# Score and probability-value matmuls issued as runs, and the next group's attention laid over eight gate tiles instead of six

## What is computed

```python
xn = rms_norm(x, lp['norm_mix'])
proj = xn @ lp['w_in']                       # q | k | v | pool_in | two gates of 1024
q, k = per-head rms_norm of q, k
a = swa_prompt(q, k, v, lp['sinks'])         # 64-query chunks see their own and the 2 chunks before
pl = pool_mixer(p_ext, pos, lp['w_pool'], lp['pool_scale'])
ya = a @ lp['w_br_attn']
yb = pl @ lp['w_br_pool']
g = jax.nn.sigmoid(gates + lp['gate_bias'])
mix = (g[:, :, 0] * ya + g[:, :, 1] * yb) @ lp['w_out']
x = x + mix
x = x + conv_ffn(rms_norm(x, lp['norm_ffn']), ...)   # up 1024->5632, conv of 3, gelu * value, down
```

## Time and profile before

| | |
|---|---|
| median of 3 runs | 3370.05 us (3366.35 to 4027.73) |
| the profiled execution | 3370.61 us |
| its span, core 6 (the slowest) | 3369.1 us |
| spans of all cores | 3351.0 to 3369.1 us |
| busy shares on core 6 | PE 97%, DVE 63%, ACT 47%, POOL 30% |

### The profile page before, as it was taken

One profiled execution on the slowest core, in us unless ns is written; L12 is line 12 of the kernel. 1 busy time (PEld: TensorE's weight loads), 2 busy tenths in 40 slices (PEclk: granted clock), 3 DMA queues, 4 the chain that ended last, 5 costly groups with the idle time before them and its releaser, 6 DMA issues.

```text
span 3369.1 us, 53769 instructions; the slowest of 8 cores (3351.0 to 3369.1 us)
## 1 busy us (share of the span) xinstructions
PE 3284.3 (97%) x17681; PEld 1605.2 (48%) x17835; DVE 2138.3 (63%) x3379; ACT 1570.1 (47%) x2557; POOL 1010.9 (30%) x1151
## 2 busy tenths in 40 slices
PE   6899999999999999999998999999999999999999
PEld 3544444444444444444444444444445555555554
DVE  4655555647766866677656555556477666776665
ACT  3444444435444654446535444444265444564444
POOL 3232323114322433234333222221143332333312
PEclk8999999999999999999998999999999999999999
DMA  9556555346422333223562222222451222112211
GB/s 192 93 113 117 115 119 113 80 155 203 115 84 67 86 90 102 83 67 73 166 188 32 77 76 76 76 76 78 154 183 57 68 68 68 34 35 68 68 45 45
DMA packets 147474, 320.45 MB, mean 95 GB/s; under 512 B 26336, under 2 KB 85376, under 8 KB 140480
## 3 DMA queue, kind: packets, MB, share of 16 engines
q1 hardware_dynamic: 134128, 214.59, 20.6%
q0 software_dynamic: 6592, 56.79, 10.9%
q10 hardware_dynamic: 6480, 45.62, 3.9%
HBM read 304.18 MB, written 115.41 MB: 125 GB/s over the span
## 4 chain that ended last, share of the span: by engine, by line
PE 90%; DMA 3%; DVE 2%; issue 2%; ACT 1%; SPq 1%; POOL 0%; DVEq 0%; ACTq 0%; POOLq 0%
PE psb L626 89%; DMA xsl<-xT 2%; SPq L642 1%; DVE xn L635 1%; DMA sph<-sph 0%; PE psb L1127 0%; ACT psb L629 0%; DVE ug L635 0%; DMA xsl<-x 0%; ACT srt L629 0%; DVE PT L632 0%; DMA xsl<-xm 0%; ACT ug L629 0%; ACT L629 0%; DVE xsl L635 0%
## 5 line engine op out<-in xcount | busy, mean ns | idle before, releaser
L626 PE MATMUL psb<-xn,w_up 128*128 128x482 bf16 (+3 forms) x6336 | 1259.2, 362 | 0.0
L626 PEld LDWEIGHTS psb<-xn,w_up 128*128 128x128 bf16 x6336 | 619.9, 98 | 636.0
L632 POOL TENSOR_TENSOR actT<-ug,uv 128x480 bf16<-128x480 f32 (+3 forms) x360 | 425.1, 1181 | 1098.5 <-ACT ug L629 939.0
L635 DVE SCALAR_TENSOR_TENSOR ug<-psb,pv,ug 128x480 f32<-128x480 f32 (+3 forms) x792 | 557.4, 704 | 128.1 <-ACT ug L629 42.2
L626 PE MATMUL psb<-actT,w_dn 128*128 128x480 bf16 (+3 forms) x3168 | 631.3, 361 | 0.0
L635 DVE SCALAR_TENSOR_TENSOR uv<-psb,pv,uv 128x480 f32<-128x480 f32 (+3 forms) x792 | 557.0, 703 | 64.2 <-ACT uv L629 11.8
L629 ACT ACTIVATE ug<-psb,pv 128x480 f32<-128x480 f32 (+3 forms) x396 | 291.8, 737 | 535.0 <-PE psb L626 523.6
L626 PE MATMUL psb<-xn,w_eg 128*128 128x512 bf16 x1969 | 476.5, 382 | 8.1 <-issue 3.0
L626 PEld LDWEIGHTS psb<-actT,w_dn 128*128 128x128 bf16 x3168 | 310.0, 98 | 315.5
L629 ACT ACTIVATE uv<-psb,pv 128x480 f32<-128x480 f32 (+3 forms) x396 | 292.7, 739 | 199.1 <-PE psb L626 198.8
L632 POOL TENSOR_TENSOR sqx<-sqx,sqx 128x512 f32<-128x512 f32 (+5 forms) x238 | 287.7, 1209 | 204.3 <-ACT sqx L629 195.9
(11 more groups left out here) (166 smaller groups left out, 2537.9 us busy)
## 6 DMA issues: line engine op xcount, KB each, us to landing
wb<-wun POOLq DMA_DIRECT2D x42, 1024.0 KB, 9.8
xsl<-x SPq DMA_DIRECT2D x68, 512.0 KB, 6.2
xm<-xsl SPq DMA_DIRECT2D x64, 512.0 KB, 5.4
xsl<-xT SPq DMA_DIRECT2D x60, 512.0 KB, 6.9
w_up<-wb ACTq DMA_DIRECT2D x22, 1024.0 KB, 5.3
xsl<-xm SPq DMA_DIRECT2D x28, 482.0 KB, 6.8
xsl<-xm SPq DMA_DIRECT2D x28, 480.0 KB, 5.0
x<-xsl SPq DMA_DIRECT2D x28, 480.0 KB, 3.2
```

Of the source, the lines that this page charges most:

```text
L626: S.op("pe", lambda e: e.matmul(out=out, lhsT=lhsT, rhs=rhs, start=start, stop=stop), reads=reads, writes=writes)
L632: S.op(eng, lambda e: e.tensor_tensor(out=out, in0=a, in1=b, op=op), reads=reads, writes=writes)
L635: S.op("dve", lambda e: e.scalar_tensor_tensor(out=out, in0=a, scalar=s, in1=b, op0=op0, op1=op1), reads=reads, writes=writes)
```

## The change

Four things. (1) `mm_run` makes one operation of the list out of several matmuls: they are issued one behind the other, with the waits ahead of the first and the signal on the last. The two matmuls of an `att_S` pair (g = 0 and 1) become one run, and the 16 of `att_PV` another. (2) The planner gives such a run its own cost (`span`): 4n/2.4 + 10, which is 223 ns for n = 128, and 580 ns for the sixteen. (3) The planner knows two modes of PE: it adds 100 ns (`SWITCH`) when it goes from a half-row run to another kind of matmul or back, and while PE is in the half-row mode it takes a half-row run that is ready ahead of all others, wherever that stands in the list. (4) In the loop over groups `att_spread` takes the place of `att_steps`: `att_S` of tile i stands behind gate tile 2i, `att_PV` of tile i behind gate tile 2i+1, and `att_T` of tile i behind gate tile 2i+2, ahead of `att_S` of tile i+1. The last `att_T` falls behind gate tile 7: it stands after the `root` and `scales` of the norm of group i+2 and ahead of `stage_F`. The attention in `stage_B` at the start of each layer keeps `att_steps`, with its matmuls in runs.

```diff
+SWITCH, RUN_PV = 100, 580.0
...
+    if op.span is not None:
+        return op.span
...
-            pick = min((x for x in pend[e] if x[0] <= t), key=lambda x: x[1])
+            half = e == "pe" and halves
+            pick = min((x for x in pend[e] if x[0] <= t), key=lambda x: (half and not x[2].half, x[1]))
...
+            if e == "pe" and op.half != halves:
+                t += SWITCH
+                halves = op.half
...
+        def mm_run(mms, reads, writes, span, half=False):
+
+            def run(e):
+                for (out, lhsT, rhs, start, stop) in mms:
+                    ins = e.matmul(out=out, lhsT=lhsT, rhs=rhs, start=start, stop=stop)
+                return ins
+            o = S.op("pe", run, reads=reads, writes=writes)
+            o.span, o.half = span, half
...
-                for g in range(2):
-                    mm(psb[0:nk, b + g, 0:4 * n].rearrange("p (h q) -> p h q", h=4), kx[g * 64:(g + 1) * 64, 0:nk],
-                       G.q[0][g * 64:(g + 1) * 64, 0:4, col - G.qo:col - G.qo + n], True, True, [kr] + G.q[1], pr(b + g))
+                mms = [(psb[0:nk, b + g, 0:4 * n].rearrange("p (h q) -> p h q", h=4), kx[g * 64:(g + 1) * 64, 0:nk],
+                        G.q[0][g * 64:(g + 1) * 64, 0:4, col - G.qo:col - G.qo + n], True, True) for g in range(2)]
+                mm_run(mms, [kr] + G.q[1], pr(b, b + 1), 4 * n / 2.4 + 10, True)
...
+            mms = []
             for g in range(2):
                 for h in range(4):
...
-                    mm(o, PT[pi][:, 0, hc:hc + n], vp[:, g, 0:65], True, False, [f"PT{pi}_0", vpr], pr(b + g))
-                    mm(o, PT[pi][0:nkc, 1, hc:hc + n], vc[0:nkc, g, 0:65], False, True, [f"PT{pi}_1", vcr], pr(b + g))
+                    mms.append((o, PT[pi][:, 0, hc:hc + n], vp[:, g, 0:65], True, False))
+                    mms.append((o, PT[pi][0:nkc, 1, hc:hc + n], vc[0:nkc, g, 0:65], False, True))
+            mm_run(mms, [f"PT{pi}_0", f"PT{pi}_1", vpr, vcr], pr(b, b + 1), RUN_PV)
...
+        def att_spread(l, G):
+
+            A = G.att
+            steps = [[] for _ in range(2 * len(A) + 1)]
+            for i, a in enumerate(A):
+                steps[2 * i].append(lambda x=a: att_S(l, G, x))
+                steps[2 * i + 1].append(lambda x=a: att_PV(l, G, x))
+                steps[2 * i + 2].insert(0, lambda x=a: att_T(l, G, x))
+            return steps
...
-                steps = att_steps(l, nxt) if nxt is not None and not (l == 0 and i == 0) else []
+                steps = att_spread(l, nxt) if nxt is not None and not (l == 0 and i == 0) else []
...
                 if job is not None:
                     job.root()
                     job.scales()
+                for st in steps[KT:]:
+                    for s in st:
+                        s()
                 for g in Gs:
                     stage_F(l, g)
```

More of the change, by code:

```diff
@@ L33 @@
                  "waits", "signal", "sig", "K", "epoch", "gidx", "chain", "alias",
-                 "preds", "after", "succ", "left", "cost", "table", "size", "shared", "start", "end")
+                 "preds", "after", "succ", "left", "cost", "table", "size", "shared", "start", "end", "span", "half")
 class _Probe:
@@ L150, in op @@
         o.chain = None
+        o.span = None
+        o.half = False
         self.ops.append(o)
@@ L226, in arrange @@
         pend = {e: [] for e in self.ENGS}
-        table, busy = None, {}
+        table, busy, halves = None, {}, False
         lock = {"dve": 0.0, "pool": 0.0}
```

## The result

The changed kernel takes 0.9887 of the time before, with a 95% interval of 0.9858 to 0.9915: 3332 us where 3370 stood, 38 us less. Two of its four runs were slow, with one die at a lower clock, and are left out; the other two took 3328.98 and 3332.22 us. The forecast was 3336, 1.0% less; it is 1.1%. The profiled execution has spans of 3318.7 to 3327.4 us over the cores, where 3351.0 to 3369.1 stood.

The account below looks back on a forecast made before the run. The prediction took PE's issue to bound the gate stage of 14 mixer groups. From 3370.6 us it took 31.9 for whole runs of four and 2.5 for the layer starts, giving 3336 us, with a range of 3322 to 3356.

Parts of the forecast that it names:

- What bounds the kernel: Gate stage of 14 mixer groups: only PE counts, busy 82.99 of 83.00 us; whatever shortens its issue is saved whole.
- The prices: Score matmuls on PE: a run of one or two costs 0.42 us, of three or four 0.64, switches included.
- The second pair and its weights: Fours in the score runs: by the skill, second pairs would wait for weight loads, 5 us off the saving; trace decides.
- Why the scores were parted: Attention tiles 2 and 3: banks come free one by one, late in the planner's reckoning, so gate matmuls go between.
- Fours everywhere: The 14 groups: four runs of four each, 35.8 us where 67.7 stands, 31.9 us saved.
- The starts: Starts of the layers: layer 0 pairs save 2.5 us, layer 1's saving falls into waits; up to 5 us either way.
- Pairs without fours: Rival, score runs: each attention tile keeps two runs of one pair, saving 20.7 us, total 3347; chance 0.12.
- Evictions: Rival, gate stage: ACT and DVE run late after the scores, half the gain lost, 16 us, total 3352; chance 0.08.
- The last transpose: Rival, fourth tile's att_T: PE waits up to 6.4 us in each of 14 groups, total 3426; chance 0.04.

Follow-up runs that it names:

- one more switch: Kernel with each tile's four score matmuls in one run, plus a full-row matmul of 32 columns between its two pairs: 0.9924, 3337.2 us.
- a parted tile: Changed kernel with a full-row matmul of 32 columns between the two halves of each score pair, spread kept: 1.0008.
- fours forced on six steps: Changed kernel with each tile's four score matmuls in one run and att_steps instead of att_spread in the gate stage: 0.9916, 3348.7 us.
- The run of four: Changed kernel with both score pairs of each attention tile in one mm_run that waits for all four banks, spread kept: 0.9886, 3323.9 us.
- the first four experiments: Runs with six steps 0.9929; spread without runs 0.9896; kernel before without table load for exponentials 0.9986; changed kernel without planner's modes 0.9887.
- the next four: Four scores in one run 0.9886; that with a small matmul between pairs 0.9924; changed kernel with halves parted 1.0008, with sixteen single operations 0.9901.

## Why the prediction was right

**What bounds the kernel.** Right. PE was and is busy for all of a later group, and what its issue lost the time lost: of the 38 us of the ratio 35 lie in the 14 groups, and 30 of these are the count of runs.

**The prices.** Right, and shown by the kernels that changed little but the count: 0.42 and 0.64 us for a run gave 23.5 where 24 came (runs without spread), 15.5 where 13.3 came (one more switch, partly by luck), 1.31 where 1.30 came (a parted tile). The cleanest check is a later group of layer 0, where PE has no gaps. Against the changed kernel's 79.7 us the prices give 2.5 us more for the kernel before, 0.6 for the runs without the spread, 0.9 for one more switch and 2.7 for the parted halves; measured are 2.5, 0.6, 0.9 and 2.6. That the second half of a pair costs nothing beside the first is shown by parting them.

**The second pair and its weights.** The row of four in 0.54 us had spoken against the Trainium skill's statement (TensorE: Matmul & The Clock Gate, section "Part 3: Packing small matmuls") that loads overlap only across row groups. The prediction left out that the same section also lets a load for the background weight buffer run ahead of matmuls in flight, so the Trainium skill speaks less clearly against the fours than the prediction says. The rows after say 0.54 again for each whole tile.

**Why the scores were parted.** The banks: right in substance, though no experiment changed the banks alone. With runs and six steps only the first tile of each group was whole; with the spread and no runs nearly all were; with fours forced on six steps PE waited for a bank. The planner's belief in table loads had a part too, 19 runs.

**Fours everywhere.** Off: 47 fours and 18 twos, not 56 fours. I followed the banks in the list for a usual group, found the first tile whole before, and took that over. In layer 1 the first tile's second pair is let in only 0.76 us and three gate matmuls later (1967.52 to 1968.28), and the group whose gate tiles alternate with those of the sample group kept two pairs in all four tiles. The run of four shows that in the later groups this was the planner's reckoning and no bank that PE would have had to wait for. The term was 31.9 and is 30.1.

**The starts.** The sum was right by luck. The 2.5 us were worked out for layer 0, where PE was taken for dense; the stretch there didn't shrink (153.1 and 153.2 us, with the cores some 6 us apart). For layer 1 the prediction had the saving fall into waits, and there the start did 2.4 us more work in the same time. The runs of half-row matmuls outside the 14 groups fell from 31 to 18 (core 7). Why they gave nothing in layer 0 wasn't tested; PE has gaps there, where a shorter issue need not show.

**Waits in the first groups.** Not foreseen: some 5 us, in the three groups where I took PE for dense because the later ones are. The miss of 1.8 in the fours goes the other way, and the forecast landed 4 us off. Why the first waits closed wasn't tested by itself. More of it came with the spread alone (6.6 us) than with the runs alone (2.2 us), which fits a lighter load on DVE and ACT there, but on core 7 one of the waits is still there; that stays open.

**The rivals.** Pairs without fours was true for nine tiles of 56. Evictions did not become the limit. The last transpose held up nothing: it stands 13 matmuls into the output projection, where the planner put it. The spread alone was not among my rivals as a theory of its own. It gives 35 of the 38 us by itself, the runs alone 24: the two do largely the same thing, they keep the scores together.

## What to carry to other kernels

Where two kinds of matmul share TensorE, count how often it goes from one to the other, not only how many there are: the busy time of the rare kind by stretch gives the count. Ahead of fusing such matmuls into one item, look at what parts them; here the banks were handed out so that the second pair got those freed last, and moving the work to other places in the list mended it without any fusing. Savings in issue count only where the engine is dense, so price each stretch by its own idle time, the first and last groups too. When you compare the lengths of stretches before and after, see that both hold the same work: here 25 matmuls had passed the mark.

## What was not expected of the hardware

On two of the three chips of the experiments the cores of one die show a granted clock that is no fall to the lower level of 1.2 GHz. All engines on core 0 of the changed kernel on the third of these chips, in the ConvFFN; the last columns are clock, DMA share and GB/s:

```profile
862.00:866.00 4.00, 4.00 (x21) 1.92 (x20) 3.90 (x7) 4.00 (x8) 3.00 (x4) 1.00 0.60 226
866.00:874.00 8.00, 8.00 (x34) 3.55 (x33) 6.31 (x10) 5.85 (x10) 7.70 (x8) 0.83 0.73 132
874.00:880.00 6.00, 6.00 (x31) 2.85 (x29) 4.80 (x8) 4.40 (x7) 4.84 (x6) 0.99 0.01 1
```

PE was busy without a gap before, during and after, and the clock fell to a mean of 0.83 for 8 us. The falls at the waits above came behind idle time instead. It recurs 16 or 17 times in the ConvFFN on the cores 0 to 3 of that chip, whose mean clocks are 0.987 to 0.989 against 0.992 to 0.994 on the others, and makes their spans 3334.6 to 3339.7 us against 3317.7 to 3325.4. The same goes on in every kernel on the chip of the first four experiments; neither the chip of the next four nor the one of the result shows it, with the same load on all cores. The Trainium skill (TensorE: Matmul & The Clock Gate, section "Part 1: The HAM clock gate") describes a limit of peak current at 13/16 of the clock for a die of which three or more cores run dense matmuls, held while the load lasts. The size fits the row; here it comes and goes while the load stays.
